# Feed-forward stage of a three-block kernel: split convolution, and up projections two chunks ahead

## The reference

```python
def causal_dwconv(x, w, bias):
    K = w.shape[0]
    s = x.shape[1]
    xp = jnp.pad(x, ((0, 0), (K - 1, 0), (0, 0)))
    out = bias
    for i in range(K):
        out = out + xp[:, i:i + s] * w[i]
    return out
...
        u = causal_dwconv(h2 @ w_up[l], ffn_conv_w[l], ffn_conv_b[l])
        u_gate, u_val = jnp.split(u, 2, axis=-1)
        x = x + (jax.nn.silu(u_gate) * u_val) @ w_down[l]
```

## Time and profile before

| what | value |
|---|---|
| three runs | 1500.94, 1501.98, 1505.4 us (median 1501.98) |
| profiled execution, span | 1502.7 us (its own time is given by the span alone) |
| TensorE busy in the span | 1318.7 us, 88% |
| VectorE busy | 977.8 us, 65% |
| ScalarE busy | 634.5 us, 42% |
| POOL busy | 589.4 us, 39% |
| last stage, from TensorE's first up matmul to the end | 1270.26 to 1502.7 us |

### The profile page before, as it was taken

One profiled execution on the slowest core, in us unless ns is written; L12 is line 12 of the kernel. 1 busy time (PEld: TensorE's weight loads), 2 busy tenths in 40 slices (PEclk: granted clock), 3 DMA queues, 4 the chain that ended last, 5 costly groups with the idle time before them and its releaser, 6 DMA issues.

```text
span 1502.7 us, 21949 instructions
## 1 busy us (share of the span) xinstructions
PE 1318.7 (88%) x7938; PEld 1130.8 (75%) x7943; DVE 977.8 (65%) x1528; ACT 634.5 (42%) x1045; POOL 589.4 (39%) x367
## 2 busy tenths in 40 slices
PE   3378799998979799999999999999899768888887
PEld 2234699997856699998788888888888657877775
DVE  7998533334774543333655666589999975788787
ACT  4301444444434554444354544355444423434433
POOL 6498444444530444443343322233332212334332
PEclk8688899999977999999799999999999979999999
DMA  7000565664300566564375423444334303354553
GB/s 230 1 29 30 179 184 183 193 182 150 111 29 1 168 195 193 174 194 142 98 229 165 138 86 87 123 142 126 112 112 140 140 28 113 113 165 149 151 164 98
DMA packets 170401, 197.04 MB, mean 131 GB/s; under 512 B 14049, under 2 KB 135397, under 8 KB 170341
## 3 DMA queue, kind: packets, MB, share of 16 engines
q1 hardware_dynamic: 169115, 192.03, 42.0%
q10 hardware_dynamic: 1226, 4.21, 0.8%
HBM read 195.17 MB, written 1.05 MB: 131 GB/s over the span
## 4 chain that ended last, share of the span: by engine, by line
PE 55%; DVE 28%; issue 7%; ACT 6%; POOL 4%; DMA 0%; ACTq 0%; DVEq 0%; POOLq 0%
PE acc L652 17%; PE wk L607 9%; PE wk L608 9%; PE wk L609 9%; DVE fp L2335 3%; DVE arena L2342 3%; ACT HI L1246 3%; DVE LO L443 2%; DVE arena L2237 2%; PE wk L884 2%; DVE arena L2185 1%; DVE arena L2221 1%; PE acc L607 1%; DVE arena L2249 1%; PE wk L1005 1%
## 5 line engine op out<-in xcount | busy, mean ns | idle before, releaser
L443 POOL TENSOR_TENSOR LO<-raw,HI 128x1024 fp32r<-128x1024 f32 (+3 forms) x191 | 455.5, 2386 | 824.2 <-ACT HI L1246 823.9
L1246 ACT ACTIVATE HI<-raw 128x1024 fp32r<-128x1024 f32 (+3 forms) x382 | 359.8, 993 | 154.8 <-PE acc L652 70.5
L607 PE MATMUL wk<-XH,HI 128*128 128x256 f32 x1296 | 376.6, 291 | 31.8 <-POOL LO L443 19.7
L608 PE MATMUL wk<-XL,HI 128*128 128x256 f32 x1296 | 371.4, 287 | 0.0
L609 PE MATMUL wk<-XH,LO 128*128 128x256 f32 x1296 | 370.9, 286 | 0.0
L443 DVE TENSOR_TENSOR LO<-raw,HI 128x1024 fp32r<-128x1024 f32 (+3 forms) x191 | 243.5, 1277 | 185.8 <-ACT HI L1246 183.6
L607 PEld LDWEIGHTS wk<-XH,HI 128*128 128x128 f32 x1296 | 253.3, 195 | 46.2 <-issue 42.9
L608 PEld LDWEIGHTS wk<-XL,HI 128*128 128x128 f32 x1296 | 253.5, 196 | 1.3
L609 PEld LDWEIGHTS wk<-XH,LO 128*128 128x128 f32 x1296 | 253.3, 195 | 0.0
L652 PE MATMUL acc<-HI,HH 128*128 128x512 f32 x424 | 135.1, 400 | 35.8 <-POOL LO L443 17.6
L652 PE MATMUL acc<-LO,HH 128*128 128x512 f32 x424 | 132.3, 393 | 0.0
(11 more groups left out here) (318 smaller groups left out, 2021.9 us busy)
## 6 DMA issues: line engine op xcount, KB each, us to landing
raw<-in_mlp_w SPq DMA_DIRECT2D x128, 512.0 KB, 4.2
raw<-in_w_in SPq DMA_DIRECT2D x100, 512.0 KB, 4.0
raw<-in_w_up SPq DMA_DIRECT2D x44, 512.0 KB, 4.5
raw<-in_w_down SPq DMA_DIRECT2D x44, 256.0 KB, 2.9
raw<-in_att_w_in SPq DMA_DIRECT2D x16, 512.0 KB, 4.1
raw<-in_w_ssd_proj SPq DMA_DIRECT2D x16, 512.0 KB, 3.6
raw<-in_att_w_out SPq DMA_DIRECT2D x8, 512.0 KB, 4.0
raw<-in_w_out SPq DMA_DIRECT2D x8, 512.0 KB, 3.4
```

The lines of the kernel that those rows point to most:

```text
L443: tensor_tensor(LO[:, s, cs], raw[:, s % 2, "ab".index(part), 0:m], HI[:, s, cs].bitcast(F32), ALU.subtract).then_inc(S(f"lo_{part}"), 1)
L607: mm(o, lh, rh, start=start, stop=False, skip_group_check=skip)
L608: mm(o, lh, rl, start=False, stop=False, skip_group_check=skip)
L1246: A(HI[:, s, j * m:(j + 1) * m], raw[:, s % 2, j, 0:m], ACT.Copy).then_inc(S(f"hi_{part}"), 1)
```

## The change

ScalarE no longer copies the bank. It reads it twice, once for gate and once for value, and writes `fconv` with the last tap's weight as scale and the bias as bias (`last_tap`). VectorE adds the other two taps straight out of PSUM with shifted ranges (`earlier_taps`), in four instructions; a range that starts two tokens or one token later takes the place of the padding. `fpad` and `fp` are gone, and so are the weights' copy and VectorE's memset. The chunk loops of ScalarE and VectorE are written out, so all addresses are constants. The conversion of pieces is put between the steps of a chunk. TensorE uses all four banks of `wk`, its loop has four chunks a turn, and the piece order is up 0, up 1, up 2, down 0, up 3, down 1, and so on.

```diff
@@ SyncE @@
             gate_val(0)
+            gate_val(1)
             with sp.Fori(0, (FC - 2) // 2) as i:
                 ring.enter(i, 1)
-                gate_val(i * 2 + 1)
+                gate_val(i * 2 + 2)
                 down1(i * 2)
-                gate_val(i * 2 + 2)
+                gate_val(i * 2 + 3)
                 down1(i * 2 + 1)
             ring.leave((FC - 2) // 2)
-            gate_val(FC - 1)
...
@@ TensorE @@
-            def ffn_up(c, par):
-                if not (isinstance(c, int) and c < 2):
-                    pe.wait_ge(S("gv_read"), c - 1)
+            def ffn_up(c, bank):
+                if not (isinstance(c, int) and c < 4):
+                    pe.wait_ge(S("fconv_ready"), c - 3)
...
-            def ffn_turn(c):
-                ffn_up(c + 1, 1)
-                ffn_down(c, 0)
-                ffn_up(c + 2, 0)
-                ffn_down(c + 1, 1)
+            def four_turns(c):
+                for j in range(4):
+                    ffn_up(c + j + 2, (j + 2) % 4)
+                    ffn_down(c + j, j % 2)
...
             ffn_up(0, 0)
             clear_acc()
-            ffn_turn(0)
...
+            ffn_up(1, 1)
+            four_turns(0)
+            with pe.Fori(0, (FC - 2) // 4 - 1) as i:
+                ring.enter(i, 2)
+                four_turns(i * 4 + 4)
+            ring.leave((FC - 2) // 4 - 1)
             ffn_down(FC - 2, 0)
             ffn_down(FC - 1, 1, True)
...
@@ ScalarE @@
+            def up_piece(c):
+                return first + (c if c < 2 else 2 * c - 2)
+
+            def down_piece(c):
+                return first + min(2 * c + 3, 2 * FC - 1)
+
+            def last_tap(c):
+                done(up_piece(c))
+                if c >= 2:
+                    act.wait_ge(S("fh_ready"), c - 1)
+                for j in range(2):
+                    last = A(fconv[:, c % 2, j, :], wk[:, c % 4, j * SEQ:(j + 1) * SEQ], ACT.Identity,
+                             bias=fpall[:, c, 4 * j + 3:4 * j + 4], scale=fpall[:, c, 4 * j + 2:4 * j + 3])
+                last.then_inc(S("ftap_ready"), 1)
...
+            def hidden_high(c):
                 act.wait_ge(S("fh_ready"), c + 1)
+                if c >= 2:
+                    done(down_piece(c - 2))
+                A(HH[:, c % 2, 0, :], fhid[:, c % 2, :], ACT.Copy).then_inc(S("f_hi"), 1)
+
+            for c in range(FC):
+                last_tap(c)
+                hi_to(down_piece(c) - 1)
+                gate_tanh(c)
+                hi_to(down_piece(c))
+                hidden_high(c)
...
@@ VectorE @@
+            def earlier_taps(c):
+                dve.wait_ge(S("ftap_ready"), c + 1)
+                for k in (1, 0):
                     for j in range(2):
...
-                    if k < 2:
+                        o = fconv[:, c % 2, j, 2 - k:SEQ]
+                        last = STT(o, wk[:, c % 4, j * SEQ:(j + 1) * SEQ - (2 - k)], fpall[:, c, 4 * j + k:4 * j + k + 1], o,
+                                   ALU.mult, ALU.add)
+                    if k == 1:
                         link(last)
                 last.then_inc(S("fconv_ready"), 1)
...
+            for c in range(FC):
+                earlier_taps(c)
+                lo_to(down_piece(c) - 1)
+                gated_hidden(c)
+                lo_to(down_piece(c))
+                hidden_low(c)
```

More of the change, by code:

```diff
@@ L144, in build @@
         fpall = sb("fpall", [P, FC, 8])
-        fp = sb("fp", [P, 2, 8])
         h = sb("h", [P, TB, D])
@@ L270, in build @@
         yn = carve(14900, 2, SEQ)
-        fpad = carve(0, 2, 2, 260)
         fconv = carve(1040, 2, 2, SEQ)
@@ L430, in size @@
                 m = n - P_WOUT2 - 4
-                return 1024 if (m in (42, 43) or (m % 2 == 0 and 2 <= m < 42)) else 2048
+                return 1024 if m == 2 * FC - 2 or (m % 2 == 1 and m > 1) else 2048
             return SMALL.get(n, 2048)
@@ L1184, in _ @@
             norm_transpose(6)
-            def ffn_up(c, par):
-                if not (isinstance(c, int) and c < 2):
-                    pe.wait_ge(S("gv_read"), c - 1)
+            def ffn_up(c, bank):
+                if not (isinstance(c, int) and c < 4):
+                    pe.wait_ge(S("fconv_ready"), c - 3)
                 s = arrived()
-                used(ch_major(s, par, True, norm=6 if isinstance(c, int) and c == 0 else None))
+                used(ch_major(s, bank, True, norm=6 if isinstance(c, int) and c == 0 else None))
             def ffn_down(c, par, end=False):
@@ L1685, in ffn, with gate_tanh @@
+            def last_tap(c):
[6 more added lines that the diff above has]
+                last.then_inc(S("ftap_ready"), 1)
+            def gate_tanh(c):
                 act.wait_ge(S("fconv_ready"), c + 1)
-                if not (isinstance(c, int) and c < 2):
-                    act.wait_ge(S("fh_ready"), c - 1)
@@ L1688, in ffn @@
-                A(ftanh[:, par, :], fconv[:, par, 0, :], ACT.Tanh).then_inc(S("ftanh_ready"), 1)
-            def ffn_hi(c, par):
+                A(ftanh[:, c % 2, :], fconv[:, c % 2, 0, :], ACT.Tanh).then_inc(S("ftanh_ready"), 1)
+            def hidden_high(c):
                 act.wait_ge(S("fh_ready"), c + 1)
[L1692 to L1714, removed]
+                if c >= 2:
[7 more added lines that the diff above has]
+                hidden_high(c)
@@ L2320, in _ @@
             lo_to(first + 1)
-            link(V.memset(fpad[:, :, :, 0:2], 0.0))
             for tb in range(TB):
@@ L2340, in ffn @@
                     for j in range(2):
-                        o, s, w = fconv[:, par, j, :], fpad[:, par, j, k:k + SEQ], [fp[:, par, 4 * j + n:4 * j + n + 1] for n in range(4)]
-                        last = TS(o, s, w[0], w[3], ALU.mult, ALU.add) if k == 0 else STT(o, s, w[k], o, ALU.mult, ALU.add)
-                    if k < 2:
+                        o = fconv[:, c % 2, j, 2 - k:SEQ]
+                        last = STT(o, wk[:, c % 4, j * SEQ:(j + 1) * SEQ - (2 - k)], fpall[:, c, 4 * j + k:4 * j + k + 1], o,
+                                   ALU.mult, ALU.add)
@@ L2344, in ffn, with gated_hidden @@
+                    if k == 1:
                         link(last)
                 last.then_inc(S("fconv_ready"), 1)
+            def gated_hidden(c):
                 dve.wait_ge(S("ftanh_ready"), c + 1)
-                link(STT(fhid[:, par, :], ftanh[:, par, :], 1.0, fconv[:, par, 0, :], ALU.add, ALU.mult))
-                TT(fhid[:, par, :], fhid[:, par, :], fconv[:, par, 1, :], ALU.mult).then_inc(S("fh_ready"), 1)
+                link(STT(fhid[:, c % 2, :], ftanh[:, c % 2, :], 1.0, fconv[:, c % 2, 0, :], ALU.add, ALU.mult))
+                TT(fhid[:, c % 2, :], fhid[:, c % 2, :], fconv[:, c % 2, 1, :], ALU.mult).then_inc(S("fh_ready"), 1)
@@ L2349, in ffn, with hidden_low @@
+            def hidden_low(c):
                 dve.wait_ge(S("f_hi"), c + 1)
-                TT(HL[:, par, 0, :], fhid[:, par, :], HH[:, par, 0, :].bitcast(F32), ALU.subtract)\
+                TT(HL[:, c % 2, 0, :], fhid[:, c % 2, :], HH[:, c % 2, 0, :].bitcast(F32), ALU.subtract)\
                     .then_inc(S("f_lo"), 1)
[L2353 to L2366, removed]
+            for c in range(FC):
[4 more added lines that the diff above has]
+                hidden_low(c)
             for tb in range(TB):
```

## The result

| | before | changed kernel |
|---|---|---|
| median, us | 1503.66 (1500.94 to 1505.4, 4 runs) | **1465.66** (1465.11 to 1466.44, 4 runs) |
| profiled execution: span | 1502.7 | 1463.2 (its own time 1465.11) |
| last stage, TensorE's first up matmul to the end | 232.4 (from 1270.26) | 193.6 (from 1269.64) |
| one chunk | 10.18 | 8.50 |
| TensorE / VectorE / ScalarE / POOL busy | 1318.7 / 977.8 / 634.5 / 589.4 | 1304.6 / 964.6 / 645.9 / 594.4 |

The ratio is 0.9743, 95% interval 0.9728 to 0.9757: 2.6% faster, 38 us. The forecast was 1463 with a range of 1460 to 1474.

The account below looks back on a forecast made before the run. VectorE's chain of waits, not TensorE's work, bounded the last stage at 10.18 us a chunk. Twenty chunks times 1.70 (34) and 5.4 at the end take 39.4 off 1502.7: 1463.3, forecast 1463, range 1460 to 1474.

Parts of the forecast that it names:

- TensorE's bound: Last stage: TensorE by itself needs 5.75 us for an up piece and 2.73 for a down piece, 8.48 a chunk.
- The weights' copy goes: VectorE's chunk cycle in the last stage: without the copy 2.35 us less, 10.18 to 7.83, below TensorE's 8.48.
- Locks: Rival in the last stage: POOL's low parts wait for VectorE's low part and product, 35.5 us more, 1499; chance 0.03.
- load chain: Up-piece loads through one slot of `raw`: 8.60 us a round beside TensorE's 8.48; as rival 1479, chance 0.09.
- VectorE's work of 5.2 us a chunk: VectorE's sum for one last-stage chunk: 1.79 + 1.46 + 0.69 and three instructions at 0.43.
- Order: Last stage, two chunks ahead: five us slack on pieces and ten on product cover TensorE's waits before down and up pieces.
- T+17: About 17 us after an up piece ends (T), when TensorE wants that chunk's product; forecast ready by about T+7.2.
- Taps: Last-stage convolution: ScalarE's two reads 0.93 against 0.58 for its copy; VectorE saves 0.81, its other four stay 1.79.
- Loads: Last-stage up-piece loads: losing 0.12 a chunk over 18 chunks uses 2.2 of 2.7 us in hand; cost 0.
- Loops: Last stage's written-out code and four-chunk turn: cost 0, upper bound 4 turns x 1 us.
- clock: Rival: 175 us without a gap granted less than full; 10% of the stage at 1.2 GHz adds 17.5, 1481; chance 0.04.
- the end: After up 21 TensorE has 5.46 us of down pieces, the last product takes 5.1: no wait, 5.4 us saved.

## Why the prediction was right, and where it was not

**TensorE's bound, right.** 5.75 + 2.73 = 8.48 was forecast and 8.50 measured, with TensorE 20.00 of 20 and nothing but matmuls on the chain. The sum rests on this. The span came out at 1463.2 against 1463.3, with some luck: the stage began 0.6 us earlier (1269.64). The profiled execution's own time is 1.9 above its span, where I had set the span 0.7 above the median; that is most of the 2.7 between 1463 and 1465.66.

**"The weights' copy goes: 2.35 off VectorE's cycle ... it alone takes the stage to TensorE's bound", wrong.** This step failed, and that the forecast of the time held in spite of it is luck as far as this step goes. The copy costs 0.17, and 2.35 beside POOL. Without it the cycle fell by 0.3 and the stage stayed at 9.88. In the earlier trace rows the evidence was there: the copy ends at 1397.19 + 2.35 = 1399.54 and POOL at 1399.51, and eight columns were booked longer than the low part of 1024 ahead of them (1.46). I read the end times beside each other only for the loop of loads. The final time didn't suffer, because the complete change passes the bound by another way.

**Locks, the mechanism right and the price in the wrong place.** This rival said that the low parts on POOL and VectorE's instructions exclude each other, and priced it as delay of POOL in the load chain, 1499. They do exclude each other, for whole instructions. But it is mostly VectorE that is held, in the kernel before on the chain that sets its pace, and in the changed kernel where it has slack. The Trainium skill, "SBUF — State Buffer", section SBUF: two separate sides, states the exclusive lock for a VectorE instruction with two SBUF inputs and also for one in a mode that uses two ports, and it has a float32 copy from SBUF to SBUF as a case of the latter. The prediction named only the first kind, and the copy is of the second. The traces agree for both: the product takes 2.63 and 1.40 beside POOL and 0.42 without, the copy 2.36 and 0.17. The first taps, with one tensor input in SBUF and two scalars, are held as well (two in 2.76 and 0.73). The taps with one tensor in PSUM and the other in SBUF are not.

**VectorE's work of 5.2 us a chunk, mis-sized.** The instructions are as forecast, but two are held, 2.63 + 1.40 in place of 2 x 0.42, 3.2 us. The cycle from one chunk's taps to the next is 1368.92 - 1360.63 = 8.29. So the margin under TensorE's 8.50 is 0.2 us and not 3.3. The product is ready some 10.8 us after its up piece's end and not 7.2 (taps of chunk 10 begin at 1359.60, 1.94 late), still before T+17: the second chunk of lead covers it.

**Order, right as cover, incomplete as cause.** Both old waits are gone. But two chunks of lead aren't needed for it: with PSUM taps, one chunk ahead also has TensorE full and waits about 2.5 us, at the end. And neither the new order alone (9.84) nor the removed copy alone (9.88) comes near the bound. What counts is which VectorE instruction stands beside POOL's low parts and who waits for it. Before, it is the copy, ahead of the convolution for which TensorE waits. In the changed kernel it is the product: the taps run from 1360.63 to 1362.41 while POOL stands idle, and POOL begins at 1363.13. With the second chunk of lead the held product still has some 6 us to spare (10.8 against 17). So there the taps gain little by reading PSUM: with six taps out of SBUF the chunk is 8.66, 0.16 more. With one chunk of lead the split convolution is worth 9.58 - 8.50 = 1.08 a chunk at least, cut off at TensorE's bound. Of that 9.58 the hold on the first taps has 3.49 - 0.73 = 2.76; without it VectorE's chain would be 6.8 by my estimate, under the bound, with all six taps still on VectorE.

**Taps.** 0.478 from PSUM, as taken, and 0.482 for the same instruction out of SBUF in the kernel before. The Trainium skill, "Perfetto Trace Analysis", section Optimizing Scalar/DVE Operations, gives PSUM the higher price on VectorE; the traces don't show it for this instruction. ScalarE's two reads cost 1.00 together in its timeline and not 0.93.

**Loads, right.** The 32 loads of `w_up` between 1300 and 1440 had 3.8 as their median, against the 4.6 that I took, so the chain had over half a microsecond to spare. **Loops, clock, the end, right**: no wait at a loop's head, a granted clock of 1.00 in every window from 1280 on (0.83 from 1270 to 1280), and the last product 1452.25 + 4.07 = 1456.32, 5.33 after up 21's end (1450.99), forecast 5.1, under a cover of 5.46. This too was closer than it looks.

**Open.** One chunk ahead, taps from PSUM and the tap on ScalarE were tried together, so their shares in the 1.08 are separated only by the estimate above and not by a run. The second chunk of lead was not put alone into the kernel before, so no run shows what it would bring there. In the kernel before without POOL, 8.89 remains where TensorE needs 8.50: VectorE's chain sets it, whose only gaps in a chunk are waits of 0.17, 0.48 and 0.48 for ScalarE.

## What to carry to other kernels

When an instruction's duration is far out of line with its size, look at what ends when it ends, on the other engines: the trace may book a wait inside an instruction as work. Price a removal only after that, since taking the instruction away can move such a wait to the next one. Beside POOL's work place VectorE instructions of the kind that were not held here (one tensor in PSUM), or ones that nobody waits for, and try whether VectorE does POOL's share faster.

## What the runs showed of the hardware that I had not expected

- A VectorE copy of 128x8 took 0.17 us with POOL idle and 2.35 with a low part on POOL (the mean of 18 copies in the kernel before is 2353 ns); in the chunks shown it ended within 0.04 us of POOL.
- Held beside POOL: the copy (2.35, alone 0.17), the first taps out of SBUF (two in 2.76 to 3.49, alone 0.73), the down piece's low part (2.51, alone 0.68), the product (2.63 and 1.40, alone 0.42). Not held: taps that read one tensor from PSUM and one from SBUF (four in 1.77 beside POOL, 1.78 alone).
- Giving VectorE POOL's work, some 1.8 us more a chunk, made the kernel before some 1.9% faster (0.9814, 0.9791 to 0.9837).
- A register in the address of the copy cost nothing that can be measured (2.35 and 2.36).
